# A hybrid attention and short-convolution layer on one core: rotary key in two products per k tile, sums and splits moved

## What is computed

```python
h  = modulate(rmsnorm(x, norm1_g), sh1, sc1)        # adaLN: shift, scale, gate from SiLU(c) @ w_ada
hc = modulate(rmsnorm(ctx, norm1_g), csh1, csc1)
p, pc = h @ w_in, hc @ w_in[:, :KR_END]             # [kv latent 256 | rope key 32 | q latent 384 | conv x, B, C | gates]
# attention: 8 heads, 64 plain + 32 rotary dimensions, one rotary key shared by all heads
k_rope = rope2d(p[..., KV_END:KR_END]); q = rmsnorm(q latent) @ w_uq; k, v = rmsnorm(kv latent) @ w_ukv
# short convolution: B * dwconv3(C * x_in), merged with the attention by two sigmoid gates, then w_o
x = x + g1 * (merged @ w_o)
x = x + g2 * conv_ffn(modulate(rmsnorm(x, norm2_g), sh2, sc2), w_up, ..., w_down)
out = rmsnorm(x, final_g)
```

## Time and profile before

| | |
|---|---|
| median of 3 runs | 836.61 us (835.13 to 836.73) |
| profiled execution | 835.09 us, span 833.1 us, mean granted TensorE clock 0.987 |
| TensorE | busy 810.3 us, 97% of the span |
| VectorE | busy 511.6 us, 61% |
| ScalarE, GpSimd | busy 370.5 and 370.7 us, 44% each |
| HBM | 95.17 MB read, mean 117 GB/s |

### The profile page before, as it was taken

How to read it: one execution, slowest core, us unless ns; L and a number is a source line. 1 busy time by engine, 2 the same in 40 slices (tenths; PEclk the granted TensorE clock), 3 DMA queues, 4 the chain that set the end, 5 groups by cost and what they waited for, 6 DMA issues and landing times. The chain is left out here.

```text
span 833.1 us, 11435 instructions
## 1 busy us (share of the span) xinstructions
PE 810.3 (97%) x3937; PEld 675.5 (81%) x3937; DVE 511.6 (61%) x652; ACT 370.5 (44%) x589; POOL 370.7 (44%) x193
## 2 busy tenths in 40 slices
PE   5899999999999999999999999999999999999997
PEld 4778877888888888888788988888888887888885
DVE  5778687688888477978204575555555556345535
ACT  7656556565666322323324664433444433221223
POOL 5315484526433554654544064444444443544430
PEclk9899999999999999999999999999999999999999
DMA  9752241101010788776263034323333321232212
GB/s 305 223 166 52 76 102 51 51 26 52 26 51 27 235 267 249 233 243 212 89 240 102 1 103 124 100 88 90 100 101 101 100 90 65 98 126 78 100 51 101
DMA packets 120289, 97.82 MB, mean 117 GB/s; under 512 B 13660, under 2 KB 106105, under 8 KB 120249
## 3 DMA queue, kind: packets, MB, share of 16 engines
q1 hardware_dynamic: 120137, 97.26, 37.8%
q10 hardware_dynamic: 112, 0.04, 0.0%
HBM read 95.17 MB, written 2.10 MB: 117 GB/s over the span
## 5 line engine op out<-in xcount | busy, mean ns | idle before, releaser
L344 POOL TENSOR_TENSOR wlo<-raw,whi 128x1024 fp32r<-128x1024 f32 (+4 forms) x125 | 282.8, 2270 | 361.5 <-ACT whi L336 361.0
L425 PE MATMUL ps<-hhi,whi 128*128 128x512 f32 (+1 forms) x520 | 196.0, 377 | 0.2 <-DVE hlo L1452 0.2
L427 PE MATMUL ps<-hhi,wlo 128*128 128x512 f32 (+1 forms) x520 | 195.6, 376 | 0.0
L426 PE MATMUL ps<-hlo,whi 128*128 128x512 f32 (+1 forms) x520 | 195.5, 376 | 0.0
L336 ACT ACTIVATE whi<-raw 128x1024 fp32r<-128x1024 f32 (+4 forms) x125 | 118.3, 958 | 139.2 <-PE ps L427 55.9
L425 PEld LDWEIGHTS ps<-hhi,whi 128*128 128x128 f32 x520 | 97.8, 188 | 18.1 <-DVE hlo L1452 0.4
L427 PEld LDWEIGHTS ps<-hhi,wlo 128*128 128x128 f32 x520 | 97.8, 188 | 18.0
L426 PEld LDWEIGHTS ps<-hlo,whi 128*128 128x128 f32 x520 | 97.9, 188 | 18.0
L1478 DVE TENSOR_TENSOR raw<-raw,gbc 128x1024 f32<-128x1024 f32 x22 | 48.7, 2214 | 47.0 <-DMA raw<-w_down_dram 47.0
L1486 DVE SCALAR_TENSOR_TENSOR work<-ps,prm,work 128x511 f32<-128x511 f32 x44 | 33.0, 749 | 71.8 <-ACT work L1035 71.0
L1385 DVE SCALAR_TENSOR_TENSOR adacc<-ada,cvec,adacc 128x1024 f32<-128x1024 f32 x28 | 64.1, 2327 | 14.3 <-DMA ada<-w_ada_dram 14.3
(11 more groups left out here) (288 smaller groups left out, 1512.2 us busy)
## 6 DMA issues: line engine op xcount, KB each, us to landing
raw<-w_up_dram SPq DMA_DIRECT2D x88, 256.0 KB, 3.1
ada<-w_ada_dram SPq DMA_DIRECT2D x32, 512.0 KB, 6.3
raw<-w_in_dram SPq DMA_DIRECT2D x56, 256.0 KB, 4.2
raw<-w_down_dram SPq DMA_DIRECT2D x44, 256.0 KB, 2.7
adaraw<-w_ada_dram SPq DMA_DIRECT2D x32, 256.0 KB, 5.5
raw<-w_o_dram SPq DMA_DIRECT2D x16, 256.0 KB, 3.0
xt<-x_dram SPq DMA_DIRECT2D x4, 512.0 KB, 7.9
raw<-w_attn_out_dram SPq DMA_DIRECT2D x8, 256.0 KB, 2.7
```

Source lines behind the costliest of these rows:

```text
L344: ins = (engine or nc.gpsimd).tensor_tensor(out=l, in0=r, in1=h.bitcast(F32), op=ALU.subtract)
L425: pe.matmul(o, l[0], r[0], start=start, stop=False)
L426: pe.matmul(o, l[0], r[1], start=False, stop=False)
L427: return pe.matmul(o, l[1], r[0], start=False, stop=stop)
```

## The change

1. **Chunk 0:** all `latents(1, ...)` tiles go behind the `mod_sums`, as in the other chunks.
2. **Rotary key:** the weight tile in `whi` holds zeros and the high part (64 + 64 columns), that in `wlo` the low part and a copy of the high part; two matmuls per k tile (`key_pair`) give lo x hi in rows 0 to 63 and the rest in rows 64 to 127. ScalarE copies rows 0 to 63 out (`kr_low`), VectorE adds them. GpSimd gets a memset per unit, ScalarE one copy more per unit. VectorE's rotation of the latent key (`rotary_key`, now four operations) stands behind head 1, its two splits behind heads 2 and 3.
3. **One-column sums:** the 4 query sums stand two by two behind k tiles 1 and 2 of head 1, the 6 key sums one by one behind the first 6 matmuls of the convolution piece. The 16 sums of the second modulation stand in groups of 3, 3, 2, 2, 2, 2, 2 in the last 24 matmuls of the merge (bank 4); `gate_rows` goes behind the merge.
4. **Query stage's splits:** unit `U_CX0` goes ahead of the latent squares, `U_UQ[2]` ahead of the scales (its low part from ahead of head 0 to behind it), `U_CC0` ahead of head 3's split.
5. **Attention:** the first `conv_taps` goes from ahead of `normalize(0)` to ahead of the first `ptlo`.
6. **FFN:** `U_UP + 2` and `+ 3` are split behind `normed2(0)` and `(1)`; in the last turn of `up` the third and fourth `gated_rows` and their splits go behind the last tile's taps.

```diff
+NORM2_SUMS = (0, 3, 6, 8, 10, 12, 14, 16)
...
-            if isinstance(u, int) and U_KR <= u < U_KR + 2:
-                return headed_raw(slot, DT // 2), headed(whi, slot, DT // 2), headed(wlo, slot, DT // 2)
...
+        def key_hi(act, u, slot):
+
+            arrived(act, u, slot)
+            wait(act, w_used, u - SLOTS + 1)
+            for r, h in zip(headed_raw(slot, DT // 2), key_parts(key_tiles(whi, slot), NOPE)):
+                if h.shape[-1] == ROPE:
+                    r = r[:, :, NOPE:QK]
+                ins = nc.scalar.activation(h, r, ACT.Copy)
+            ins.then_inc(w_hi, 1)
+            act.wait_ge(w_hi, u + 1)
+            nc.scalar.activation(key_tiles(wlo, slot)[:, :, NOPE:P], key_tiles(whi, slot)[:, :, NOPE:P], ACT.Copy).then_inc(s("kr_both"), 1)
...
+        def key_lo(pool, u, slot):
+
+            wait(pool, w_used, u - SLOTS + 1)
+            nc.gpsimd.memset(key_tiles(whi, slot)[:, :, 0:NOPE].bitcast(F32), 0.0).then_inc(s("kr_zero"), 1)
+            pool.wait_ge(w_hi, u + 1)
+            pool.wait_ge(s("kr_zero"), u - U_KR + 1)
+            for r, h, l in zip(headed_raw(slot, DT // 2), key_parts(key_tiles(whi, slot), NOPE), key_parts(key_tiles(wlo, slot), 0)):
...
+                ins = nc.gpsimd.tensor_tensor(out=l, in0=r, in1=h.bitcast(F32), op=ALU.subtract)
+            ins.then_inc(w_lo, 1)
...
-                    sp.wait_ge(s("cols2_ps"), 1)
+                    sp.wait_ge(s("gbc_ps"), 4)
...
-            for u in range(U_KR, U_UQ[2] + 1):
+            for u in range(U_KR, U_KR + 2):
+                key_lo(pool, u, u % SLOTS)
+            for u in range(U_KR + 2, U_UQ[2]):
...
+                if h == 3:
+                    split_lo(pool, U_CC0, U_CC0 % SLOTS)
...
-                if h in (1, 3, 4, 5):
-                    u = {1: U_UQ[3], 3: U_CC0, 4: U_V, 5: U_N}[h]
+                if h in (0, 1, 4, 5):
+                    u = {0: U_UQ[2], 1: U_UQ[3], 4: U_V, 5: U_N}[h]
                     split_lo(pool, u, u % SLOTS)
...
-                split_hi(act, u, u % SLOTS)
+                key_hi(act, u, u % SLOTS)
...
+            for u in (*U_UQ[0:2], U_CX0):
                 split_hi(act, u, u % SLOTS)
 
+            used(act, U_KR + 1)
+            nc.scalar.activation(krot2[NOPE:P, :], ps[0:NOPE, 3, :], ACT.Copy).then_inc(s("kr_low"), 1)
+            nc.scalar.activation(kr_ctx[NOPE:P, :], ps[0:NOPE, 0, 0:C], ACT.Copy).then_inc(s("kr_low"), 1)
...
-            split_hi(act, U_CX0, U_CX0 % SLOTS)
...
-                split_hi(act, U_UQ[2], U_UQ[2] % SLOTS)
...
+                if h == 3:
+                    split_hi(act, U_CC0, U_CC0 % SLOTS)
...
+                if h in (0, 1, 4, 5):
+                    u = {0: U_UQ[2], 1: U_UQ[3], 4: U_V, 5: U_N}[h]
+                    split_hi(act, u, u % SLOTS)
...
-                if h in (1, 3, 4, 5):
-                    u = {1: U_UQ[3], 3: U_CC0, 4: U_V, 5: U_N}[h]
-                    split_hi(act, u, u % SLOTS)
...
-            for m in range(SLOTS):
+            for m in range(2):
...
+                split_hi(act, U_UP + 2 + t, 2 + t, free=U_O + t + 3)
...
+                        if not (last and jj == 1):
+                            split_hi(act, U_UP + 4 * i + 2 * jj + n + 4, 2 * jj + n, gated=2 * jj + n if last else None)
+                    if last and jj == 1:
+                        for n in range(2):
+                            split_hi(act, U_DOWN + 2 + n, 2 + n, gated=2 + n)
...
-            dve.wait_ge(s("kr_ps"), 1)
-            dve.wait_ge(s("tab_loaded"), 16)
-            kr, tmp = krot[NOPE:QK, :], krot2[NOPE:QK, :]
-            kr_ps, kr_ctx = ps[:, 3, :], ps[:, 0, 0:C]
-            nc.vector.tensor_tensor(out=kr_ps[NOPE:QK, :], in0=kr_ps[NOPE:QK, :], in1=tab[NOPE:QK, :], op=ALU.mult).then_inc(s("kr"), 1)
...
+            kr, low = krot[NOPE:QK, :], krot2[NOPE:P, :]
+            dve.wait_ge(s("q_sum"), QT - 1)
             used(dve, U_KR + 1)
-            nc.vector.tensor_tensor(out=tmp, in0=kr_ps[QK:P, :], in1=tab[QK:P, :], op=ALU.mult).then_inc(s("kr"), 1)
-            nc.vector.tensor_copy(kr[:, T:K], kr_ctx[NOPE:QK, :]).then_inc(s("kr"), 1)
-            dve.wait_ge(s("kr"), 3)
-            nc.vector.tensor_tensor(out=kr[:, 0:T], in0=kr_ps[NOPE:QK, :], in1=tmp, op=ALU.add).then_inc(s("kr"), 1)
+            dve.wait_ge(s("kr_low"), 2)
+            nc.vector.tensor_tensor(out=kr[:, T:K], in0=ps[NOPE:QK, 0, 0:C], in1=kr_ctx[NOPE:QK, :], op=ALU.add).then_inc(s("kr"), 1)
...
+            def rotary_key():
+
+                dve.wait_ge(s("tab_loaded"), 16)
+                nc.vector.tensor_tensor(out=ps[NOPE:P, 3, :], in0=ps[NOPE:P, 3, :], in1=low, op=ALU.add).then_inc(s("kr"), 1)
+                dve.wait_ge(s("kr"), 2)
+                nc.vector.tensor_tensor(out=krot2[QK:P, :], in0=ps[QK:P, 3, :], in1=tab[QK:P, :], op=ALU.mult).then_inc(s("kr"), 1)
+                nc.vector.tensor_tensor(out=ps[NOPE:QK, 3, :], in0=ps[NOPE:QK, 3, :], in1=tab[NOPE:QK, :], op=ALU.mult).then_inc(s("kr"), 1)
+                dve.wait_ge(s("kr"), 4)
+                nc.vector.tensor_tensor(out=kr[:, 0:T], in0=ps[NOPE:QK, 3, :], in1=krot2[QK:P, :], op=ALU.add).then_inc(s("kr"), 1)
...
+                if h == 1:
+                    rotary_key()
+                if h in (2, 3):
+                    rotary_key_split(h - 2)
...
-                if h in (1, 2):
-                    rotary_key_split(h - 1)
...
             maxima(1)
-            conv_taps(0)
             normalize(0)
...
                     normalize(g + 1)
+                if g == 0:
+                    conv_taps(0)
+                    dve.wait_ge(s("c_tap"), 2)
                 dve.wait_ge(s("pt_hi"), 2 * g + 1)
...
+            def norm2_mods():
+
+                dve.wait_ge(s("cols2_ps"), 1)
...
                 if d == DT - 1:
-                    gate_rows()
+                    norm2_mods()
...
+            gate_rows()
...
-                        if last:
-                            gated_rows(2 * jj + n, 2 * jj + n)
+                        if last and jj == 0:
+                            gated_rows(n, n)
+                    if last and jj == 1:
+                        for n in range(2):
+                            gated_rows(2 + n, 2 + n)
...
-                if c_ == 0:
-                    latents(1, (0, 1))
...
-                    latents(2 * c_ + 1, (0,) if c_ else (2,))
+                    latents(2 * c_ + 1, (0,))
                     mod_columns(c_ + 1)
-                    latents(2 * c_ + 1, (1, 2, 3, 4) if c_ else (3, 4))
+                    latents(2 * c_ + 1, (1, 2, 3, 4))
...
+            def key_pair(o, slot, k, hi, lo):
+
+                at = slice(k % 4 * P, (k % 4 + 1) * P)
+                pe.matmul(o, wlo[:, slot, at], hi[:, k, :], start=k == 0, stop=False)
+                return pe.matmul(o, whi[:, slot, at], lo[:, k, :], start=False, stop=k == DT - 1)
...
-                last = project(pe, ps[:, 3, :], u % SLOTS, hhi[:, 4 * n:4 * n + 4, :], hlo[:, 4 * n:4 * n + 4, :], kt=DT // 2,
-                               start=n == 0, stop=n == 1)
-            last.then_inc(s("kr_ps"), 1)
+                pe.wait_ge(s("kr_both"), n + 1)
+                for k in range(4 * n, 4 * n + 4):
+                    key_pair(ps[:, 3, :], u % SLOTS, k, hhi, hlo)
...
-                last = mm3(pe, ps[:, 0, 0:C], (tile_of(whi, u % SLOTS, k % 4), tile_of(wlo, u % SLOTS, k % 4)),
-                           (chi[:, k, :], clo[:, k, :]), k == 0, k == DT - 1)
+                last = key_pair(ps[:, 0, 0:C], u % SLOTS, k, chi, clo)
...
+            def query_sum(t):
+
+                if t == 0:
+                    pe.wait_ge(s("q_sum"), QT - 1)
+                    pe.wait_ge(s("p_raw"), KVT)
+                last = pe.matmul(ps[:, 6, t:t + 1], work[:, 3, t * P:(t + 1) * P], ones[:, 0:1], start=True, stop=True)
+                if t == TT - 1:
+                    last.then_inc(s("q_stat"), 1)
+
+            def key_sum(t):
+
+                if t == 0:
+                    pe.wait_ge(s("k_ssq"), 1)
+                last = pe.matmul(ps[:, 6, 8 + t:9 + t], sqk[0][:, t * P:(t + 1) * P], ones[:, 0:1], start=True, stop=True)
+                if t == KT - 1:
+                    last.then_inc(s("stat_ps"), 1)
...
+                    if i - at < sums:
+                        key_sum(i - at)
...
-                last.then_inc(s("q_ps") if h % 2 == 0 else w_used, 1)
-                if h == 1:
-                    pe.wait_ge(s("p_raw"), KVT)
-                    latent_sums()
+                    if k == QT - 1:
+                        last.then_inc(s("q_ps") if h % 2 == 0 else w_used, 1)
+                    if h == 1 and k > 0:
+                        query_sum(2 * k - 2)
+                        query_sum(2 * k - 1)
                 if 1 <= h < 4:
-                    conv_piece(0, 0, 8 * (h - 1), 8)
+                    conv_piece(0, 0, 8 * (h - 1), 8, KT if h == 1 else 0)
...
                 pe.wait_ge(s("m_prod"), 2 * DT - 2)
```

(25 more changed lines are left out.)

44 lines of the change are left out of this document (20 added, 24 removed).

## The result

| | before | changed |
|---|---|---|
| median, run beside each other | 836.44 us (834.11 to 837.27, 8 runs) | 840.04 us (837.77 to 841.29, 8 runs) |
| ratio, 95% interval | 1 | 1.0049 (1.0037 to 1.0061) |
| TensorE | busy 810.3 of 833.1 us | busy 809.0 of 838.1 us |

What follows compares the result with a forecast made beforehand. TensorE's matmul list, its idle places and low-clock stretches were taken as the bound. Terms -0.3 + 1.5 - 1.2 - 1.4 = -1.4 took the profiled 835.09 to 833.7, or 835.2 as median; range 831.0 to 838.5.

Steps and rivals of the forecast that it cites:

- Chunk 0: Start of kernel: six moved matmuls cover VectorE's `hhi`/`hlo`, so TensorE's idle of 0.97 us goes; -1.0 us.
- Rotary key: Key's products: two instead of three save TensorE 2.8 us, but it then idles 0.9 for `cqlo`; -1.9 from key to head 0.
- Query stage: Head 0 to first scores: TensorE idles about 1.5 us for `p_raw`, VectorE's list grows; most earlier gain is handed over.
- steps 1 to 3: Chunk 0, rotary key and query stage together, at the first scores: -0.3 us, between -1.3 and +1.4.
- of the 3.6 idle it can use about 2.6: Query stage: VectorE's added work was to fill about 2.6 of its 3.6 us idle time.
- The sign that the prediction had named: Key's splits at 2 us each and `cklo` ending after 121.5 would show the forecast wrong.
- First taps: Attention: taps ahead of `ptlo` lengthen TensorE's idle before `transposes(1)` from 0.7 to 2.2 us; +1.5 us.
- rival B: Longer idle places before `transposes(1)` and the values bring new clock falls, 1.65 us each; 838.5 with two; chance 0.20.
- Merge: Spread sums remove the clock's fall after the sixteen sums (-1.7), six more small-to-big returns cost 0.5; -1.2 us.
- Rival C: Spread one-column sums don't keep the clock, so the fall at the merge may stay; 836.9 us; chance 0.13.
- Last turn of `up`: FFN: gated rows and splits behind the last taps remove TensorE's 1.4 us wait before `down`; -1.4 us.
- Rival A: VectorE and ScalarE keep TensorE's pace, so up to the first scores -3 to -5.7; 832.5, at best 829.8; chance 0.27.

Runs made afterwards that it cites:

- e4_splits_early: Changed kernel with VectorE's two splits of the rotary key behind heads 1 and 2 instead of 2 and 3; 836.34 us, ratio 1.0017.
- e2_sums_grouped: Changed kernel with the query stage's ten one-column sums together behind head 1, as before; 837.45 us, ratio 1.0033.
- e10_three_and_splits: Kernel before with only the change's chunk 0 order, merge and FFN edits, plus its places for the UQ2 and CC0 splits; 829.18 us, ratio 0.9929.
- e5_mended: Changed kernel with first taps ahead of `normalize(0)`, ten sums together behind head 1, key's splits behind heads 1 and 2; 831.76 us, ratio 0.9958.
- e7_rotary_ahead: e5_mended with the latent key's rotation of four operations back ahead of head 0; 831.74 us, ratio 0.9959.

## Why the prediction was wrong, point by point

**Chunk 0** (forecast -1.0, measured -1.26): right, the wait of 0.97 is gone in all twelve profiles with this order. The stretch as a whole varied from 49.6 to 50.4 us in them, so the 0.26 beyond the forecast mean nothing.

**Rotary key** (-1.9, measured -1.46): right in kind. The products gave 2.65 us; the wait for `cqlo` was forecast at 0.9 and is 1.03, and the step across it (74.97 to 76.39) is 1.42, which is 1.19 more than a step without a wait.

**Query stage: the step that failed.** It gave -0.3 for steps 1 to 3 at the first scores, with a worst case of +1.4; measured from the first latents it was +5.8 (4.8 in the two profiles' own times, which the terms below use). Its first half was right: ScalarE's p_raw is 89.18 (forecast 89.8), the wait 1.70 (1.5), and VectorE's heads begin at 89.25 (89.8). Two terms in it were wrong:

- I chose -0.3 near the good end "since TensorE is ahead", and in TensorE's own list I counted the old fall of the clock behind the sums as gone (-1.65). It was 3.67 ahead at head 0, but the wait took 1.7 of it, the low clock over 10 us instead of 3.4 took 3.4 more, and VectorE's head 3 began at 106.48, 1.50 later than before.
- The key's splits were priced as "0 to 1.1 more" for contention, as if their place in VectorE's list cost nothing. The second one left a place with idle time for a stretch that has none, so its own length counted, and both its operations met long ones of GpSimd: 4.3 us. That is 3.5 more between head 3 and the end of VectorE's last query, net of 0.8 idle us. 1.5 + 3.5 = the 5.0 us by which the last query came later. e4_splits_early, which undoes this alone, shows the second term; e2_sums_grouped the first.

In the terms of the forecast, the row that failed is "of the 3.6 idle it can use about 2.6". From VectorE's first head to the end of `cklo`, its start came 2.28 earlier, its work grew by 4.1, and its idle time, instead of shrinking by 2.6, grew by 3.1: -2.28 + 4.11 + 3.13 = 4.96. The sign that the prediction had named came too: splits near 2 us (2.36 and 1.92) and `cklo` ending after 121.5 (at 125.60).

The second split took 4.28 us beside GpSimd's low parts; behind head 2 in e4_splits_early it took 1.77. The Trainium skill says that VectorE and GpSimd lock each other out of a shared port, and that copies and casts can be among the operations that do ("SBUF — State Buffer", "Who interferes with whom"); the trace agrees. The prediction had applied it to the low part alone.

What sets the length is what GpSimd had still to run when VectorE's operation began. Over all fourteen profiles, each cast of the key that began while an operation of GpSimd was running ended 0.41 to 0.44 us behind the end of that one (16 of 16), each low part of the key 0.81 or 0.82 us behind it (17 of 17); with none running they took 0.54 or 0.55, and 0.95. (Three began within 0.02 us of one: two casts took 0.79 and 0.81, a low part 0.95.) So the prediction read its two rows, 0.95 and 2.06, only half right: the operation of 0.95 stood beside a low part of GpSimd too, but had begun first. And the change made the collision itself: it moved CC0's low part, one operation of 2.41 us, to where it started 0.47 us ahead of the cast. In e4_splits_early and e10_three_and_splits the split met pieces of 0.4 to 1.4 us.

**First taps** (+1.5, measured +1.57 on this stretch): the wait grew to 2.53 (2.2 forecast). The mechanism of **rival B**, a fall of the clock behind it, came in all five profiles with that order: another 1.6. I had given it 0.20. Its time of 838.5 is too low by what the query stage lost.

**Merge** (-1.2, measured -1.21 - 0.15): right as a sum, with luck. The fall that goes was priced at -1.7 and the output product gained 1.21; the returns were priced at +0.5 and the merge measured -0.15. The two misses nearly cancel, and no run says why the returns cost nothing there. The output product took 290.4 us in both profiles of before and 289.2 in all twelve with the new merge, at full clock. **Rival C** fell there. In head 1 its doubt was justified: low clock stayed behind the spread sums. But grouped sums behind a like wait had it as well (e5_mended, e7_rotary_ahead), so spreading alone was not its cause. **Last turn of `up`** (-1.4, measured -1.64): right.

**Rival A** fell: VectorE did not keep pace.

All stretches but head 0 to the first scores and the fall behind the taps were forecast at -4.0 and came to -4.15; single terms missed by up to 0.65 and cancelled, so the closeness is partly luck. The range missed because its upper end held one or two falls, or a VectorE late by 1.7, never a VectorE late by 5 beside them.
